# Two blocks of a language model on one core: the second block's attention and cell steps placed by half unit of its projections

## The reference, cut to what matters

```python
def token_mixer(h, w_in, ml_conv_w, ml_conv_b, ml_i_b, ml_f_b, ml_norm_g, attn_sinks, attn_norm_g, w_out):
    proj = h @ w_in
    qk_ml, v_ml, o_ml, gates, q_at, kv_at = jnp.split(proj, cuts, axis=-1)
    qk_ml = jax.nn.silu(causal_dwconv(qk_ml, ml_conv_w, ml_conv_b))      # q, k of the cell
    i_pre = gates[..., :ML_H] + ml_i_b
    logf = jax.nn.log_sigmoid(gates[..., ML_H:] + ml_f_b)
    h_ml = mlstm_chunkwise(q_ml, k_ml / sqrt(128), v_ml, i_pre, logf)
    h_ml = rms_norm(h_ml, ml_norm_g) * jax.nn.sigmoid(o_ml)
    o_at = sliding_window_attention(rope(q_at), rope(k_at), v_at, attn_sinks)
    o_at = rms_norm(o_at, attn_norm_g)
    return jnp.concatenate([h_ml, o_at], axis=-1) @ w_out

# attention, per block of 128 queries and its band of 256 keys
    s = q @ k.T / sqrt(64), masked to the band
    m = maximum(max(s), sink)
    p = exp(s - m);  p = p / (sum(p) + exp(sink - m));  o = p @ v
# cell, per chunk: scores of the chunk times a decay, plus the state C times q; then C is updated
```

## Time and profile before

| what | value |
|---|---|
| median of 3 runs | 1898.7 us (1897.71 to 1898.96) |
| the profiled execution's own time | 1899.32 us |
| its span | 1897.5 us |
| mean granted TensorE clock, whole span | 0.943 |
| TensorE busy | 1704.9 us (90%) |
| VectorE, ScalarE, GpSimd busy | 874.3, 637.6, 799.2 us |
| stretch of the changed steps, GA to the start of WO | 1187.5 to 1424.95 us |

### The profile page before, as it was taken

One profiled execution on the slowest core, in us unless ns is written; L12 is line 12 of the kernel. 1 busy time (PEld: TensorE's weight loads), 2 busy tenths in 40 slices (PEclk: granted clock), 3 DMA queues, 4 the chain that ended last, 5 costly groups with the idle time before them and its releaser, 6 DMA issues.

```text
span 1897.5 us, 20659 instructions
## 1 busy us (share of the span) xinstructions
PE 1704.9 (90%) x7616; PEld 1368.1 (72%) x7616; DVE 874.3 (46%) x1153; ACT 637.6 (34%) x827; POOL 799.2 (42%) x639
## 2 busy tenths in 40 slices
PE   3988999999979997999999987788869699999995
PEld 1666788787857885788888856667757377888884
DVE  5536455544484344543343455552561655203424
ACT  3534434343223223431143222443222434324331
POOL 1263555455444553455445523232134145444441
PEclk7988999999989998999999988897879799999998
DMA  8111112122324541345534531111002033232221
GB/s 308 45 67 45 67 67 89 67 89 89 122 82 166 185 177 68 131 142 185 186 136 153 178 133 48 64 50 62 23 23 71 22 130 126 76 120 89 84 92 58
DMA packets 35234, 195.22 MB, mean 103 GB/s; under 512 B 3904, under 2 KB 4032, under 8 KB 19648
## 3 DMA queue, kind: packets, MB, share of 16 engines
q1 hardware_dynamic: 23616, 151.96, 22.3%
q10 hardware_dynamic: 11520, 41.95, 6.4%
HBM read 191.80 MB, written 2.10 MB: 102 GB/s over the span
## 4 chain that ended last, share of the span: by engine, by line
PE 70%; DVE 14%; ACT 6%; POOL 5%; issue 3%; DMA 1%; DVEq 0%; SPq 0%; ACTq 0%; POOLq 0%
PE main L717 54%; PE main L713 8%; POOL w_lo L561 4%; ACT w_hi L1018 2%; DVE rstd L1591 1%; PE auxB L741 1%; DVE tmp L1391 1%; DVE h_lo L1621 1%; DVE tmp L1531 1%; PE auxD L820 1%; DMA ada_first<-w_ada 1%; DVE x L1606 1%; DVE ysum L1605 1%; DVE tmp L1730 1%; PE auxD L733 1%
## 5 line engine op out<-in xcount | busy, mean ns | idle before, releaser
L561 POOL TENSOR_TENSOR w_lo<-raw,w_hi 128x512 fp32r<-128x512 f32 (+1 forms) x525 | 707.6, 1379 | 903.8 <-ACT w_hi L1018 903.6
L717 PE MATMUL main<-h_hi,w_hi 128*128 128x512 f32 (+1 forms) x1144 | 460.4, 402 | 44.5 <-POOL w_lo L561 16.9
L717 PE MATMUL main<-h_lo,w_hi 128*128 128x512 f32 (+1 forms) x1144 | 451.9, 395 | 0.0
L717 PE MATMUL main<-h_hi,w_lo 128*128 128x512 f32 (+1 forms) x1144 | 451.7, 395 | 0.0
L1018 ACT ACTIVATE w_hi<-raw 128x2048 fp32r<-128x2048 f32 (+3 forms) x136 | 249.3, 1833 | 261.2 <-PE main L717 222.4
L717 PEld LDWEIGHTS main<-h_hi,w_hi 128*128 128x128 f32 (+1 forms) x1144 | 218.0, 191 | 110.1 <-issue 27.7
L717 PEld LDWEIGHTS main<-h_hi,w_lo 128*128 128x128 f32 (+1 forms) x1144 | 217.5, 190 | 48.3 <-issue 1.0
L717 PEld LDWEIGHTS main<-h_lo,w_hi 128*128 128x128 f32 (+1 forms) x1144 | 218.5, 191 | 42.9
L1531 DVE SCALAR_TENSOR_TENSOR tmp<-main,par,tmp 128x511 f32<-128x511 f32 x88 | 65.9, 749 | 176.3 <-ACT tmp L1107 174.7
L1556 DVE SCALAR_TENSOR_TENSOR ada_acc<-ada_raw,cs,ada_acc 128x1024 f32<-128x1024 f32 x70 | 115.3, 1648 | 29.2 <-DMA ada_raw<-w_ada 21.3
L713 PE MATMUL main<-w_hi,h_hi 128*128 128x512 f32 (+1 forms) x256 | 105.6, 412 | 19.8 <-POOL w_lo L561 10.2
(11 more groups left out here) (329 smaller groups left out, 2390.8 us busy)
## 6 DMA issues: line engine op xcount, KB each, us to landing
raw<-stream SPq DMA_DIRECT2D x119, 1024.0 KB, 4.9
ada_raw<-w_ada ACTq DMA_DIRECT2D x80, 512.0 KB, 4.2
ada_first<-w_ada SPq DMA_DIRECT2D x16, 512.0 KB, 6.8
raw<-stream SPq DMA_DIRECT2D x8, 768.0 KB, 4.1
raw<-stream SPq DMA_DIRECT2D x8, 640.0 KB, 3.8
x<-x_in SPq DMA_DIRECT2D x2, 2048.0 KB, 10.6
out<-x SPq DMA_DIRECT2D x8, 256.0 KB, 2.0
con<-consts SPq DMA_DIRECT2D x1, 486.0 KB, 3.7
```

Of the source, the lines that this page charges most:

```text
L561: ins = nc.gpsimd.tensor_tensor(w_lo[:, s, a:b], raw[:, s, a:b], w_hi[:, s, a:b], ALU.subtract)
L717: ins = nc.tensor.matmul(bank[0:n, :], w[:, k, col:col + n], a[:, ka_, :], start=start, stop=stop)
```

## The change

- GA's unit holds both gate groups in one tile (4 columns at row 0, 4 at row 32): 36 columns instead of 256, one job of 24 matmuls instead of two. VectorE copies both rows out and adds the biases in place.
- Rotated queries 0 and 1 are turned behind GA; 2 and 3 between the halves of QK 0. The gate steps are cut in three: `ml_gates` behind GA, `ml_scan` (VectorE) in the middle of QK 0, `ml_exp` (ScalarE) behind it.
- With slots counted in half units from the middle of QK 0 (slot 0), attention step q has its scores in slot q, its transposes in slot q+2 and its output in slot q+3, so one step starts per half unit. Odd q use a second pair of buffers, laid into the four tiles of `og`, which the output gate writes only in O1. `att` has four sets of small columns. Square and power of query block i are a step of their own (`att_square`, slot 2i+5), one half unit behind the block's second output, and the scaling is another (`att_norm`, slot 2i+6); both were inside `att_out`.
- `k_turn` 0 to 3 are in slots 6 to 9. Cell scores c are in slot 10+c (the first in the middle of V1) and `ml_out` c in slot 11+c, so the last is in the middle of O1. Each waits only for its own value tile.
- Within a slot the new list `rank` sorts the steps: transposes, output, scores, `k_turn`, cell output, cell scores.
- `join` multiplies the output gate chunk by chunk instead of four at once.

```diff
@@ -98,7 +98,7 @@
     u += [Unit("KV", "w_in_2", 0, KD, [(KV2, 256, 0)], "h", token_major=True)]
     u += [Unit(f"QA{i}", "w_in_2", 4 * i, 4, [(QA2, 512, 0)], "h", ak0=4 * i, token_major=True,
                first=(i == 0), last=(i == 1)) for i in range(2)]
-    u += [Unit("GA", "w_in_2", 0, KD, [(GATES2, MH, P - MH), (GATES2 + MH, MH, P - MH)], "h")]
+    u += [Unit("GA", "w_in_2", 0, KD, [(GATES2, MH, 32 - MH), (GATES2 + MH, MH, 0)], "h")]
...
     mid[at["QA0"][0]] += [("rope_k", 0)]
-    mid[at["GA"][0]] += [("rope_q", 0), ("rope_q", 1)]
-    end[at["GA"][0]] += [("rope_q", 2), ("rope_q", 3), ("ml_gates", 0)]
+    end[at["GA"][0]] += [("rope_q", 0), ("rope_q", 1), ("ml_gates", 0)]
+    mid[at["QK"][0]] += [("rope_q", 2), ("rope_q", 3), ("ml_scan", 0)]
+    end[at["QK"][0]] += [("ml_exp", 0)]
     mid[at["QK"][1]] += [("ml_columns", 0)]
     for hd in range(MH):
-        (end, mid)[hd % 2][at["QK"][3] + (hd + 1) // 2].append(("k_turn", hd))
-    n = at["GA"][0]
+        slot(2 * at["QK"][3] + hd).append(("k_turn", hd))
+    first = 2 * at["QK"][0]
     for q in range(2 * TC):
-        end[n + q + 1].append(("att_out", q))
-    for q in range(2 * TC):
-        mid[n + q + 1].append(("att_turn", q))
-        end[n + q].append(("att_scores", q))
-    end[at["V1"][0]] += [("ml_scores", 0)]
-    mid[at["O0"][0]] += [("ml_out", 0), ("ml_scores", 1)]
-    end[at["O0"][0]] += [("ml_out", 1), ("ml_scores", 2)]
-    mid[at["O1"][0]] += [("ml_out", 2), ("ml_scores", 3)]
-    before[at["WO"][0]] += [("ml_out", 3)] + [("join", c) for c in range(TC)]
+        slot(first + q).append(("att_scores", q))
+        slot(first + q + 2).append(("att_turn", q))
+        slot(first + q + 3).append(("att_out", q))
+    for i in range(TC):
+        slot(first + 2 * i + 5).append(("att_square", i))
+        slot(first + 2 * i + 6).append(("att_norm", i))
+    for c in range(TC):
+        slot(2 * at["V1"][0] + c).append(("ml_scores", c))
+        slot(2 * at["V1"][0] + c + 1).append(("ml_out", c))
+    before[at["WO"][0]] += [("join", c) for c in range(TC)]
     before[at["FU"][0]] += square_sums(4, at["WO"]) + [("norm", 4)] + all_sums(5) + [("norm", 5)]
     last = square_sums(6, at["FD"][9::2]) + [("norm", 6)]
     for p, n in enumerate(ada_slots(at)):
@@ -264,7 +266,8 @@
         if p % 8 == 7:
             end[n].append(("ada_sum", p // 8 + 2))
 
-    rank = ["silu", "b_turn", "ssd_out", "ssd_scores", "xs_turn", "ssd_turn"]
+    rank = ["silu", "b_turn", "ssd_out", "ssd_scores", "xs_turn", "ssd_turn", "rope_q", "ml_columns", "att_turn", "att_out",
+            "att_scores", "k_turn", "ml_out", "ml_scores"]
...
+        probs = [prob[:, :, :], og[:, 0:2, :].rearrange("p a (j k) -> p (a j) k", k=2 * P)]
+        probs_t = [prob_t[:, :, :, :], og[:, 2:4, :].rearrange("p a (j r k) -> p (a j) r k", r=2, k=P)]
...
-            def att_out(q, n):
-                if q % 2 == 0:
-                    return
-                i = q // 2
+            def att_square(i, n):
+                st = att[:, i % 4, :]
                 pool.wait_ge(at_sq, i + 1)
-                link(nc.gpsimd.tensor_scalar(att[:, 26:27], att[:, 25:26], 1.0 / (AH * AD), RMS_EPS, ALU.mult, ALU.add))
-                nc.gpsimd.tensor_tensor(att[:, 27:28], att[:, 26:27], small[:, 63:64], ALU.pow).then_inc(at_rs, 1)
+                link(nc.gpsimd.tensor_scalar(st[:, 26:27], st[:, 25:26], 1.0 / (AH * AD), RMS_EPS, ALU.mult, ALU.add))
+                nc.gpsimd.tensor_tensor(st[:, 27:28], st[:, 26:27], small[:, 63:64], ALU.pow).then_inc(at_rs, 1)
...
-                pe.wait_ge(v_ready, TC)
+                pe.wait_ge(v_ready, c + 1)
...
             def att_scores(q, n):
                 ks = slice(P, 2 * P) if q < 2 else slice(0, 2 * P)
                 act.wait_ge(sm_max, q + 1)
+                pr, st = probs[q % 2], att[:, q % 4, :]
                 for j in range(4):
-                    run_act(prob[:, j, ks], prob[:, j, ks], ACT.Exp, bias=att[:, 8 + j:9 + j], accum_out=att[:, 12 + j:13 + j])
-                run_act(att[:, 16:20], att[:, 16:20], ACT.Exp).then_inc(sm_exp, 1)
+                    run_act(pr[:, j, ks], pr[:, j, ks], ACT.Exp, bias=st[:, 8 + j:9 + j], accum_out=st[:, 12 + j:13 + j])
+                run_act(st[:, 16:20], st[:, 16:20], ACT.Exp).then_inc(sm_exp, 1)
 
             def att_turn(q, n):
                 rs_ = 1 if q < 2 else 0
-                if q:
-                    read_by_pe(("att_out", q - 1), 0)
+                if q >= 2:
+                    read_by_pe(("att_out", q - 2), 0)
                 for b in range(2):
                     bank, free = full(("att_turn", q), b)
-                    link(run_act(prob_t[:, 2 * b:2 * b + 2, rs_:2, :],
+                    link(run_act(probs_t[q % 2][:, 2 * b:2 * b + 2, rs_:2, :],
                             bank[:, :].rearrange("p (j r t) -> p j r t", j=2, r=2)[:, :, rs_:2, :], ACT.Copy))
                     act.sem_inc(free, 1)
                     act.sem_inc(pt_ready, 1)
 
-            def att_out(q, n):
-                if q % 2:
-                    i = q // 2
-                    act.wait_ge(at_raw, q + 1)
-                    read_by_pe(("ml_columns", 0), 0)
-                    if i:
-                        act.wait_ge(at_rs, i)
-                    run_act(quant[:, :], qa[:, i, :, :].rearrange("p t d -> p (t d)"), ACT.Square,
-                            accum_out=att[:, 25:26]).then_inc(at_sq, 1)
+            def att_square(i, n):
+                act.wait_ge(at_raw, 2 * i + 2)
+                read_by_pe(("ml_columns", 0), 0)
+                run_act(quant[:, :], qa[:, i, :, :].rearrange("p t d -> p (t d)"), ACT.Square,
+                        accum_out=att[:, i % 4, 25:26]).then_inc(at_sq, 1)
...
                 elif u.name == "GA":
                     bank, free = tile(j)
-                    link(ts((row_i, row_f)[t], bank[0:MH, :], pc("gate_b", t, t + 1)[0:MH, :], None, ALU.add))
+                    nc.vector.tensor_copy(row_i, bank[0:MH, :])
+                    link(nc.vector.tensor_copy(row_f, bank[32:32 + MH, :]))
                     dve.sem_inc(free, 1)
+                    ts(row_i, row_i, pc("gate_b", 0, 1)[0:MH, :], None, ALU.add)
+                    link(ts(row_f, row_f, pc("gate_b", 1, 2)[0:MH, :], None, ALU.add))
...
+                pr, st = probs[q % 2], att[:, q % 4, :]
+                if q >= 2:
+                    full(("att_turn", q - 2), 1)
...
-                    for k in range(TC):
-                        stt(hm[:, k, :], og[:, k, :], 1.0, hm[:, k, :], ALU.add, ALU.mult).then_inc(ml_out, 1)
+                stt(hm[:, c, :], og[:, c, :], 1.0, hm[:, c, :], ALU.add, ALU.mult).then_inc(ml_out, 1)
```

More of the change, by code:

```diff
@@ L381, in build @@
             dec = alloc(s5, "dec", [MH * TC])
-            att = alloc(s5, "att", [32])
+            att = alloc(s5, "att", [4, 32])
             decb = alloc(s5, "decb", [MH * TC])
@@ L884, in att_out_ @@
                             continue
-                        ins = nc.tensor.matmul(bank[:, AD * j:AD * (j + 1)], prob_t[:, j, r, :],
+                        ins = nc.tensor.matmul(bank[:, AD * j:AD * (j + 1)], probs_t[q % 2][:, j, r, :],
                                                va[:, i - 1 + r, AD * g:AD * (g + 1)], start=(r == 0 or i == 0), stop=(r == 1))
@@ L1777, in ml_gates, with ml_scan @@
                 dve.sem_inc(mg_x, 1)
+            def ml_scan(i, n):
+                scan = nc.vector.tensor_tensor_scan
                 dve.wait_ge(mg_e, 1)
@@ L1821, in ml_scores @@
                 dve.sem_inc(ml_p, 1)
-                dve.wait_ge(v_ready, TC)
+                dve.wait_ge(v_ready, c + 1)
                 vw = flat_tmp(SEQ, MH * W).rearrange("p (h d) -> p h d", h=MH)
```

43 lines of the change are left out of this document (23 added, 20 removed).

## The result

The changed kernel takes 1903.95 us (median of 16 runs, 1900.61 to 1907.29), the kernel before 1898.88 in the same comparison. The profiled execution took 1904.24 us, with a span of 1902.4 against 1897.5.

What follows compares the result with a forecast made beforehand. TensorE bounds the kernel, losing time to waits and a low clock. Terms -8.4+15.8+19.6-3.5-25.2 give -1.7, plus 2.5 for clock: +0.8 on 1899.32, or 1900.1; the median is 0.6 lower, 1899.5 us. Range 1890 to 1909, the forecast's own 1896 to 1903.

Steps and rivals of the forecast that it cites:

- the allowance for the clock in slots 3 to 5: Attention slots 3 to 5: low clock behind waits of 2.0 to 2.7 us, taken as 2.5 us between 0 and 9.9.
- the one fall in the earlier trace: Kernel before: clock of 0.50 after a 1.9 us wait for auxB, the ground for taking a quarter of 9.9 us.
- halves between 5.5 and 7.5 in the cell slots: Cell slots: 8.0 us of steps plus a half unit of 5.5 to 7.5, taken as 15.0 a slot, three times.
- the -1.7: Whole changed stretch, GA to WO: sum of the stage terms, -8.4+15.8+19.6-3.5-25.2 us, before the 2.5 clock allowance.
- The clock falls in every attention slot: Rival: slots 3 to 5 cost 9.9 instead of 2.5, scores in 6 and 7 slow too; 1910.7 us, chance 0.34.
- The clock holds: Rival: half the low clock counted in slots 2, 6, 7 and cell steps stays away; 1891 us, chance 0.20.
- The copies come early: Rival: scores find their banks free and exponentials precede the keys, minus five times 2.0 us; 1889.5 us, chance 0.08.
- my -8.4 for that stage: Gates and QK 0: 30.2 us from GA's start to QK 0's end against 38.6 before, including 5.5 fewer for matmuls.
- One sign of mine: Joins: the profile after would show WO starting 13 to 14 us behind the last half of O1.
- the sum's 26.0: Last half, heads and joins: heads ready 12.6 us behind that slot's start, then 13.4 to WO.
- Gating by chunk, which I had at -0.7: Joins: from first gating to WO 13.4 us instead of 14.1, at 2.9 per chunk.

Runs made afterwards that it cites:

- the two runs with the fill: Changed kernel with ten idle matmuls per slot in slots 2 to 7, ahead of the scores (1891.22 us) or behind them (1913.73 us).
- the first experiment: Changed kernel with ScalarE's copies of transposed probabilities in slots 2 to 7 moved between the tile's first tap and its tanh: 1885.29 us, ratio 0.9935.

## Why the prediction was right or wrong

The forecast was 1899.5 us, within 0.2% of before. The measured 1903.95 lies inside the prediction's range of 1890 to 1909 and just outside the forecast's own, 1896 to 1903. How near it came is partly luck: one term was 11.5 us too small and another 6.1 too large. The stretch by the prediction's own cuts, in us from the start of GA (the prediction calls the cuts at 1261.6, 1305.8 and 1328.8 the middle of QK 2, V0 and V1; by the trace they are the ends of these units, and the sum is the same):

| stage | before | predicted | measured | what decided |
|---|---|---|---|---|
| gates, QK 0 | 38.6 | 30.2 | 31.8 | the 7.1 wait for query 3 came as said, the half behind it took 7.8, not 6.2 |
| to the end of QK 2 (slots 1 to 4) | 35.5 | 51.3 | 60.9 | waits as said, clock 0.72 |
| to the end of V0 (slots 5 to 8) | 44.2 | 63.8 | 65.2 | key waits of 5.5 as said, clock in slot 5 |
| to the end of V1 (slots 9, 10) | 22.9 | 19.4 | 18.5 | |
| cell slots (11 to 13) | 96.2, with the next row | 45.0 | 38.9 | clock 1.00, 13.0 a slot instead of 15.0 |
| last half, heads, joins | in the row above | 26.0 | 27.8 | 3.3 per chunk instead of 2.9 |
| sum | 237.4 | 235.7 + 2.5 | 243.1 | |

**The term that was sized wrong** is the allowance for the clock in slots 3 to 5: "Bounds: never, 0; each time, 3.3 us a slot ... 9.9. I take 2.5, a quarter". It fell in every one. The three slots took 16.5, 17.1 and 15.2 where I had 12.2, 12.9 and 12.2, 11.5 us more, beyond even my upper bound, since the half units behind the waits took up to 8.4 and I had counted 7.1. The reason I gave for the small value, that the one fall in the earlier trace rows had thin work on both sides, was wrong: in these slots the work around is dense, and the two runs with the fill showed that it is the wait that counts. My reading of the earlier trace rows was weak too. The window 1380 to 1382, which I took for a clock of 1.00 after the 1.5 us wait, lies inside that wait, which ended at 1382.07. Behind it the clock did hold, but it fell in the next half unit, behind a wait of 0.94 (kernel before):

```profile
1382.00:1384.00 2.00, 1.80 (x13) 1.61 (x14) 0.58 (x2) 0.00 (x0) 2.00 (x3) 1.00 0.00 0
1388.80:1390.80 2.00, 2.00 (x7) 1.62 (x7) 1.91 (x3) 0.00 (x0) 0.00 (x0) 0.70 0.00 0
```

The waits themselves were near: 2.0 to 3.3 us in slots 3 to 5 against 2.0 to 2.7, two of 5.5 for the keys against 5.4, and 3.0 ahead of `ml_columns` where I had said 4 to 5. The end of QK 3 came 37.6 us later than before (1315.9 against 1278.3), where I had said some 25.

**What paid it back** is an error of the other sign. I expected halves between 5.5 and 7.5 in the cell slots by the earlier trace rows; with the attention steps gone from them TensorE waits there less than 1 us at a time, and the clock stayed at 1.00 from 1345 to 1403. 6.1 us came back: 3.7 in the halves, which took 5.7 to 5.8 each, and the rest in the steps, 7.2 a slot instead of 8.0. The full clock is not assured by the short waits. With the same steps and waits in these three slots (0.5 and 0.9 us), one half took 7.2 to 7.4 us in the traces of eight of the nine other kernels that keep them; only the one that gates four chunks first had none. The cell slots of the first experiment, 40.0 us at a clock of 0.96:

```profile
1343.90:1383.89 39.99, 34.97 (x194) 29.29 (x194) 29.36 (x66) 6.46 (x8) 9.77 (x12) 0.96 0.08 27
```

What decides in which slot it falls, or that it does not, no run shows. Together with 1.6 in the gates, 1.1 in slot 2, -1.4 in slot 6, -0.2 in slots 7 and 8, -0.9 in slots 9 and 10 and 1.8 in the joins, the two terms make 7.4 on top of the -1.7, or 5.7 for the stretch; the span grew by 4.9.

**The rivals.** "The clock falls in every attention slot" is what happened, with its steps: slots 3 to 5 throughout, and part of the scores of slots 6 and 7 (auxC 1.67 to 1.69 instead of 1.02). Its price for that was 1910.7; that the kernel came out at 1904 is due to the cell slots. "The clock holds" was right for the cell slots alone. "The copies come early" did not occur, but the first experiment, which makes them come early, gave 17 us where I had priced it at 10: I had left the clock out.

**The parts.** The gates' smaller tile is worth nothing alone (0.9992): my -8.4 for that stage was near as a length (-6.8), but by this run it came mostly from steps that left the stage, not from the 24 matmuls. No run moves these steps alone. The cell steps' new places are worth 9 us: about 5 without the slower halves of the run that puts them back, the rest clock. One sign of mine contradicted my own sum. I wrote that WO starts 13 to 14 us behind the last half of O1. That half ended 9.9 us behind the start of its slot, so the sum's 26.0 gives 16; measured were 18.0. Gating by chunk, which I had at -0.7, costs 0.9 in the trace. VectorE's gating stands between two turns there. For chunk 0 it takes 0.69; beside GpSimd's subtraction it takes 1.53 for chunk 1 and 1.10 for each of the last two:

```profile
1418.08 1.53 DVE L1885 SCALAR_TENSOR_TENSOR hm<-og,hm 128x512 f32<-128x512 f32 x1 [0.24 <-DVE tmp L1892]
```

```profile
1417.80 2.94 POOL L625 TENSOR_TENSOR h_lo<-tmp,h_hi 128x512 fp32r<-128x512 f32 x2 [3.03 <-ACT h_hi L1320]
```

The run of the changed kernel with the old places of the cell steps measures the rest of the change: 1.0074, some 14 us slower than before. The gates' tile and the gating by chunk could not be told from no change by time, so nearly all of these 14 us are the attention pipeline with its key turns.

The Trainium skill ("Perfetto Trace Analysis", Optimizing Tensor Performance, Matmuls) asks for different banks for independent groups; the waits of slots 2 to 7 bear it out. The first experiment adds that an earlier copy out of the same bank took the waits from 15.3 to 4.0 us; no run here uses another bank. The Trainium skill ("TensorE: Matmul & The Clock Gate", A second HAM failure mode) tells of another kernel whose clock swings between its two levels because TensorE idles briefly between groups of matmuls that cycle through banks. The trace agrees: waits of 2.0 to 3.3 us, each with low clock behind it.

## What to carry to other kernels

Where TensorE waits a couple of microseconds in each turn of a loop, count the matmuls behind the wait at the lower clock as well: here 11 us of waits in four slots took another 12 of clock with them. To find out which it is, fill the wait with matmuls into a bank that is overwritten anyway; if the kernel gets faster with more work, it is the clock. Then look on the engine that is waited for: a gap in its own program, here 2.44 us between two instructions of a tile, is often where the awaited copy can go for nothing.
